# The experts' weighted rows: gather, multiply and add on VectorE, or multiply on ScalarE and add in the scatter

## What is computed

```python
xt = hn.reshape(N, D)                       # N = 1024 tokens, D = 1024
g_sel = jnp.argmax(g_logits, axis=-1)       # one of 4 groups
top_val, top_loc = lax.top_k(e_in, TOP_K)   # 2 of its 8 experts
gates = jax.nn.softmax(top_val, axis=-1) * g_gate
...
hb = jax.nn.silu(xb @ w_e_gate[e]) * (xb @ w_e_up[e])      # (rows, 256)
return (hb @ w_e_down[e]).astype(jnp.float32) * wts[:, None]
...
out = jnp.zeros((N + 1, D), jnp.float32).at[tok_buf].add(yb.reshape(P, D))[:N]
```

## Time and profile before

| | us |
|---|---|
| time, median of 3 runs (lowest to highest) | 1071.8 (1071.31 to 1072.05) |
| the profiled execution's own time | 1072.77 |
| its span in the profile | 1070.9 |
| TensorE busy | 971.1 (91%) |
| VectorE busy | 774.2 (72%) |
| ScalarE busy | 464.9 (43%) |
| GpSimd busy | 325.7 (30%) |

### The profile page before, as it was taken

The page is one execution under the profiler, slowest core; times in us unless marked ns, Lnnn a source line. Parts: engine busy times, 40 slices in busy tenths (PEclk is TensorE's granted clock), DMA queues, the critical chain, the costliest instruction groups (busy, mean ns, idle before and its releaser), DMA issues.

```text
span 1070.9 us, 13353 instructions
## 1 busy us (share of the span) xinstructions
PE 971.1 (91%) x4709; PEld 757.7 (71%) x4709; DVE 774.2 (72%) x1265; ACT 464.9 (43%) x812; POOL 325.7 (30%) x339
## 2 busy tenths in 40 slices
PE   5998989888889798999998999975999999999993
PEld 4776766556677676668876888864777777777772
DVE  5647776887787577883256677687888888888881
ACT  5234452223344423332034343343666676667650
POOL 2234114321441322210021111014245554555422
PEclk9999998998999898999999999986999999999997
DMA  7232233112232422516020111675899999999981
GB/s 250 70 92 78 92 126 99 60 59 79 80 99 89 157 90 97 159 59 226 20 85 20 40 60 60 260 293 193 334 374 399 402 400 408 408 402 405 406 287 57
DMA packets 63395, 197.38 MB, mean 184 GB/s; under 512 B 16416, under 2 KB 22976, under 8 KB 50912
## 3 DMA queue, kind: packets, MB, share of 16 engines
q1 hardware_dynamic: 43344, 152.73, 38.7%
q0 software_dynamic: 18688, 39.52, 10.4%
q10 hardware_dynamic: 1296, 4.26, 1.0%
HBM read 190.17 MB, written 37.75 MB: 213 GB/s over the span
## 4 chain that ended last, share of the span: by engine, by line
PE 67%; DVE 16%; issue 9%; ACT 2%; POOL 2%; DMA 1%; SPq 0%; ACTq 0%; DVEq 0%; POOLq 0%
PE bank L953 10%; PE bank L954 9%; PE bank L955 9%; PE gu_ps L953 5%; PE gu_ps L955 5%; PE gu_ps L954 5%; PE y_ps L1335 5%; PE xg_ps L1300 3%; DVE Wl L1778 2%; PE bank L1024 2%; PE bank L1227 1%; PE y_ps L955 1%; PE y_ps L954 1%; PE y_ps L953 1%; PE bank L1112 1%
## 5 line engine op out<-in xcount | busy, mean ns | idle before, releaser
L953 PE MATMUL bank<-Wh,hTh 128*128 128x512 f32 x384 | 156.2, 407 | 0.0
L1761 DVE TENSOR_TENSOR egl<-egr,ghi 128x2048 fp32r<-128x2048 f32 x64 | 143.9, 2288 | 14.2 <-ACT ghi L1405 14.2
L954 PE MATMUL bank<-Wl,hTh 128*128 128x512 f32 x384 | 151.0, 393 | 0.0
L955 PE MATMUL bank<-Wh,hTl 128*128 128x512 f32 x384 | 151.0, 393 | 0.0
L1405 ACT ACTIVATE ghi<-egr 128x2048 fp32r<-128x2048 f32 x64 | 119.7, 1934 | 0.0
L953 PE MATMUL gu_ps<-ghi,xgH 128*128 128x512 f32 x256 | 104.3, 408 | 1.4 <-DVE xgL L2143 1.4
L955 PE MATMUL gu_ps<-ghi,xgL 128*128 128x512 f32 x256 | 101.5, 396 | 0.0
L954 PE MATMUL gu_ps<-egl,xgH 128*128 128x512 f32 x256 | 101.0, 395 | 0.0
L953 PEld LDWEIGHTS bank<-Wh,hTh 128*128 128x128 f32 x384 | 73.5, 191 | 16.5 <-issue 2.1
L955 PEld LDWEIGHTS bank<-Wh,hTl 128*128 128x128 f32 x384 | 73.0, 190 | 15.9
L2475 POOL DMA_INDIRECT partial_rows<-pg,idh x28 | 47.5, 1695 | 119.9 <-DVE pg L2168 119.9
(11 more groups left out here) (328 smaller groups left out, 2092.8 us busy)
## 6 DMA issues: line engine op xcount, KB each, us to landing
egr<-w_e_gate SPq DMA_DIRECT2D x32, 1024.0 KB
egr<-w_e_up SPq DMA_DIRECT2D x32, 1024.0 KB
edr<-w_e_down SPq DMA_DIRECT2D x32, 1024.0 KB, 12.5
raw<-w_in SPq DMA_DIRECT2D x50, 256.0 KB, 3.0
xn<-w_in SPq DMA_DIRECT2D x22, 256.0 KB, 2.9
x_sb<-x_prompt SPq DMA_DIRECT2D x8, 512.0 KB, 6.0
partial_rows<-x_sb ACTq DMA_DIRECT2D x8, 512.0 KB, 2.7
raw<-w_xkv SPq DMA_DIRECT2D x14, 256.0 KB, 3.7
```

What stands on the lines that cost most here:

```text
L953: pe.matmul(dst, ah, bh, start=first, stop=False)
L954: pe.matmul(dst, ah, bl, start=False, stop=False)
L955: return pe.matmul(dst, al, bh, start=False, stop=last)
L1761: tt(egl[n % 4][:, a, :, :], egr[n % 4][:, a, :, :], ghi[n % 2][:, a, :, :].bitcast(F32), ALU.subtract)\
```

## The change

`add_rows` leaves VectorE. ScalarE gets `weigh_rows(n-1)`, between hidden_silu(n) and down_high(n+1), and once more at the end: it writes y_ps times the gate into `pg`, without an addend. `gather_sums` is gone. `store_rows` and `out_rows` scatter with `compute_op=ALU.add`, so that the DMA adds the rows to what stands in DRAM. Since two experts that lie four apart share tokens, the scatter of expert n waits on GpSimd until that of expert n-4 has landed; `weigh_rows(n)` waits for the same before it overwrites the buffer.

```diff
--- before.py
+++ after.py
@@ -569,7 +569,6 @@
         g_used = sem("g_used")
         d_used = sem("d_used")
         xg_ld = [sem(f"xg_ld{i}") for i in range(3)]
-        pg_ld = [sem(f"pg_ld{i}") for i in range(4)]
         xg_full = sem("xg_full")
         xg_high = sem("xg_high")
         xg_low = sem("xg_low")
@@ -1662,6 +1661,15 @@
                 copy(hbF[:, :], hb_ps[:, P:2 * P])
                 copy(hbH[:, 0, :], hb_ps[:, 0:P]).then_inc(hb_high, 1)
 
+            def weigh_rows(n):
+                e = expert(n)
+                if n == 0:
+                    act.wait_ge(meta_done, 1)
+                act.wait_ge(d_used, n + 1)
+                if n > 3:
+                    act.wait_ge(px_st[n % 4], 16 * (n // 4))
+                copy(pg[n % 4][:, :], y_ps[:, :], scale=gate_s[:, e:e + 1]).then_inc(ey_done, 1)
+
             down_high(0)
             act.wait_ge(ids_done, 1)
             act.wait_ge(g_in, 1)
@@ -1680,9 +1688,11 @@
                     gate_high(n + 1, 0)
                     gate_high(n + 1, 1)
                 hidden_silu(n)
+                weigh_rows(n - 1)
                 if n + 1 < NE:
                     down_high(n + 1)
             hidden_high(NE - 1)
+            weigh_rows(NE - 1)
 
             def more_first():
                 act.wait_ge(g_used, NE)
@@ -2159,15 +2169,6 @@
                 dve.wait_ge(hb_high, n + 1)
                 tt(hbL[:, 0, :], hb_ps[:, 0:P], hbH[:, 0, :].bitcast(F32), ALU.subtract).then_inc(hb_low, 1)
 
-            def add_rows(n):
-                e = expert(n)
-                if n == 0:
-                    dve.wait_ge(meta_done, 1)
-                dve.wait_ge(d_used, n + 1)
-                dve.wait_ge(pg_ld[n % 4], 16 * (n // 4 + 1))
-                stt(pg[n % 4][:, :], y_ps[:, :], gate_s[:, e:e + 1], pg[n % 4][:, :], ALU.mult, ALU.add)\
-                    .then_inc(ey_done, 1)
-
             def gate_values():
 
                 dve.wait_ge(g_exp, 1)
@@ -2232,7 +2233,6 @@
                     gate_low(n + 1, 0)
                     gate_low(n + 1, 1)
                 hidden(n)
-                add_rows(n - 1)
                 if n + 1 < NE:
                     down_low(n + 1)
                 if n == 2:
@@ -2240,7 +2240,6 @@
                 if n == 3:
                     half_rows()
             hidden_low(NE - 1)
-            add_rows(NE - 1)
 
             def more_first():
 
@@ -2471,6 +2470,11 @@
                                                in_offset=bass.IndirectOffsetOnAxis(ap=idx, axis=0),
                                                bounds_check=bound, oob_is_err=False)
 
+            def add_rows(table, idx, frm, bound):
+                return pool.indirect_dma_start(out=table, out_offset=bass.IndirectOffsetOnAxis(ap=idx, axis=0), in_=frm,
+                                               in_offset=None, bounds_check=bound, oob_is_err=False,
+                                               compute_op=ALU.add)
+
             def spread_rows(table, idx, frm, bound):
                 return pool.indirect_dma_start(out=table, out_offset=bass.IndirectOffsetOnAxis(ap=idx, axis=0), in_=frm,
                                                in_offset=None, bounds_check=bound, oob_is_err=False)
@@ -2481,24 +2485,20 @@
                     pool.wait_ge(xg_full, 2 * n - 4)
                 fetch(xg[n % 3][:, :], hn_dram, idh[:, e:e + 1], last_row).then_inc(xg_ld[n % 3], 16)
 
-            def gather_sums(n):
-                e = expert(n)
-                if n > 3:
-                    pool.wait_ge(px_st[n % 4], 16 * (n // 4))
-                fetch(pg[n % 4][:, :], px_dram, idh[:, e:e + 1], last_row).then_inc(pg_ld[n % 4], 16)
-
             def store_rows(n):
                 e = expert(n)
                 pool.wait_ge(ey_done, n + 1)
-                spread_rows(px_dram, idh[:, e:e + 1], pg[n % 4][:, :], last_row).then_inc(px_st[n % 4], 16)
+                if n > 3:
+                    pool.wait_ge(px_st[n % 4], 16 * (n // 4))
+                add_rows(px_dram, idh[:, e:e + 1], pg[n % 4][:, :], last_row).then_inc(px_st[n % 4], 16)
 
             def out_rows(n):
                 e = expert(n)
                 pool.wait_ge(ey_done, n + 1)
                 pool.wait_ge(copied, 16 * NT)
                 pool.wait_ge(halves_done, 1)
-                spread_rows(out[0][0], idp[:, e:e + 1], pg[n % 4][:, :], last_half).then_inc(out_st, 16)
-                spread_rows(out[1][0], ids[:, e:e + 1], pg[n % 4][:, :], last_half).then_inc(out_st, 16)
+                add_rows(out[0][0], idp[:, e:e + 1], pg[n % 4][:, :], last_half).then_inc(out_st, 16)
+                add_rows(out[1][0], ids[:, e:e + 1], pg[n % 4][:, :], last_half).then_inc(out_st, 16)
 
             pool.wait_ge(ids_done, 1)
             gather_rows(0)
@@ -2506,8 +2506,6 @@
             for i in range(NT):
                 pool.wait_ge(x_st[i % TPS], 16 * (i // TPS + 1))
             gather_rows(2)
-            for n in range(4):
-                gather_sums(n)
             gather_rows(3)
             gather_rows(4)
             for n in range(1, NE):
@@ -2515,8 +2513,6 @@
                     store_rows(n - 2)
                 if n + 4 < NE:
                     gather_rows(n + 4)
-                if 2 < n < NE - 1:
-                    gather_sums(n + 1)
             for n in range(NE - 4, NE):
                 out_rows(n)
             pool.wait_ge(out_st, 16 * 8)
```

## The result

The changed kernel took 1078.74 us (median; 1078.46 to 1081.39), the kernel before 1071.55 beside it: ratio 1.0073, 95% interval 1.0051 to 1.0094. Two further measurements gave 1.0066 (1.0047 to 1.0086) and 1.0102 (1.0083 to 1.0122). So it is 0.8% slower, some 9 us; +12.8 us was forecast. The profiled execution took 1081.39 us.

The account below looks back on a forecast made before the run. TensorE, busy all 50.00 of 50 us in mid-loop, was taken to set the pace, with transfers beside it at their limit. Loop +10.0 and tail +2.8 gave +12.8 over the median 1071.8: 1084.6 us, range 1072 to 1099.

Parts of the forecast that it names:

- The chain and its room: Expert loop: from down's end through ScalarE's first ghi, egl twice and ehb to turn_hidden; ehb may be 0.26 us late.
- ScalarE's price: ScalarE's new 128x1024 operation, right behind down's end and ahead of dhi, delays the chain by 0.96 us (0.86 to 1.28).
- Every second expert: Expert loop: TensorE's stop of 0.70 us (0.60 to 1.02) returns at every second expert, as the next chain fits.
- H_2: Place of turn_hidden(2) behind the end of down(1); TensorE's first stop there, 0.70 us.
- H_3: Place of turn_hidden(3) behind down(2)'s end, in the period with VectorE's counts; a stop of 0.97 us, 0.79 before.
- Loop: All TensorE stops over the expert loop together: +10.0 us (8.7 to 14.1).
- The adding scatter at twice a plain one: Expert loop's transfers: an adding scatter costs 2 plain ones (bounds 1 and 4), taking what the gather gave back; term nothing.
- The steady landing: Expert loop: a sign of being right, the time edr's weight loads take to land stays steady.
- room for a factor of 2.5: Expert loop's transfers: at 402 GB/s an adding scatter may take 2.5 times a plain one.
- The rival in which transfers take over: Expert loop: adding scatter beyond a factor of about 2.8, weights come too late; 1106 us at factor 4; chance 13%.
- the tail: Kernel's end: dearer issues of the adding output scatters +1.5, their longer landing +1.3; +2.8 us (0 to about 8).
- The rival "not slower": Expert loop: VectorE paces the chain, so taking 1.28 us off it removes TensorE's stop; 1070.8 us; chance 13%.

Follow-up runs that it names:

- between the ghi, last six in place: Changed kernel with ScalarE's multiplication between the two ghi copies for experts 0 to 25, in the changed kernel's place for 26 to 31; ratio 1.0046.
- the transfers alone: Changed kernel's adding scatter without the gather of partial sums, but VectorE multiplies y_ps by the gate and ScalarE is as before; ratio 1.001.
- gather kept: Adding scatter with VectorE multiplying and ScalarE as before, plus the gather of partial sums kept, its data unused; ratio 1.0155.

## Why the prediction was right, and where it was off

- **The chain and its room: shown.** The 0.26 us of room was read from the single stop of the trace before. Three delays bear it out: 0.95 us gave 0.68 per stop, 0.54 us gave 0.25, and the multiplication moved between the two ghi, expected to stop 0.27, gave 0.34 (9.95+9.83 for 19.44).
- **ScalarE's price.** Taken as 0.96, measured 1.01 from the new operation to dhi; but it began 0.05 to 0.06 us sooner behind down's last matmuls than dhi had, so the net delay is 0.95.
- **Every second expert: shown.** The two periods together take 20.12 us against 19.44, so 0.68 per stop where 0.70 was forecast; H_2 0.63 for 0.70, H_3 1.03 for 0.97. Loop +9.7 against +10.0.
- **The adding scatter at twice a plain one: shown**, 2.05 by engine time. The guess from a gather plus a scatter was close by luck as much as by reason; no row before the change had it. The Trainium skill, Collectives: The Full Stack (The bandwidth ceiling), puts the price of a reducing transfer between ranks down to two source reads; the factor of 2.05 here agrees with that.
- **The steady landing: so, but by the slower loop.** edr's stays at 11 us. With the same transfers and a period of 9.72 it grows to 14.2 and 15.7, and the prediction's own sum leaves no room there: 3.13+0.26+2x0.26 = 3.91 MB, all that 402 GB/s move in 9.72 us. Its room for a factor of 2.5 was worked out for a period of 9.72+0.35. The rival in which transfers take over was nearer than its 13% suggests: it came with one gather more.
- **The failed term is the tail, +2.8 forecast and 0 to +0.3 measured.** The issue was even dearer than taken (1.55 for 1.30), and the last one ends 10.25 behind H_31 where it was 8.97, +1.3. But the time from store(27)'s issue to the copies was shorter, not longer: 1031.64 to 1036.34, 4.7 us where it was 7.5. The term had priced the adding and taken the rest of the landing as before. But how long a transfer takes to land follows from the loop's pace. The kernel with a 128x1024 copy more on ScalarE shows it; it gathers and scatters as before and is only slower:

```profile
1032.74 1.01 POOL L2478 DMA_INDIRECT partial_rows<-pg,idh  x1 [8.02 <-DVE pg L2171]
```

```profile
1036.07 2.50 SPq L934 DMA_DIRECT2D y_prompt<-partial_rows  x4
```

There it is 3.3 us. All kernels, in the order of edr's landing (us):

| kernel | H_1 to H_31 | landing of edr, 950 to 1000 | store(27) to the copies |
|---|---|---|---|
| copy 128x1024 more | 301.3 | 9.5 | 3.3 |
| changed, plain scatters | 301.2 | 9.8 | 4.1 |
| changed | 301.3 | 11.3 | 4.7 |
| copy 128x512 more | 295.4 | 11.3 | 4.2 |
| between the ghi, last six in place | 296.6 | 12.5 | 6.9 |
| between the ghi | 296.0 | 13.0 | 5.6 |
| before | 291.6 | 14.2 | 7.5 |
| the transfers alone | 291.6 | 14.2 | 6.9 |
| dhi on VectorE | 291.2 | 15.7 | 7.8 |
| gather kept | 302.5 | 23.8 | 13.2 |

The adding itself costs 0.6 of the 4.7 (4.1 with plain scatters); dropping the gather is not what shortened it, since the kernel with the copy keeps it. So the copies started earlier against H_31 (22.6 us for 18.7), GpSimd waited 1.27 us for the last multiplication, and the dearer issues lay in that room. The kernels with the transfers alone and with dhi on VectorE, whose loop is as fast as before and whose copies start 19.6 and 18.9 us ahead, do pay 1 to 3 us. The term would have been near its mark if the loop had not lost time: loop and tail don't add up independently. The other part is behind the last issue: 10.4 us to the end where it was 11.5, although the adding output scatters land 3.9 to 4.2 us after their issue and the plain ones 2.4 to 2.5 (second trace of the kernel before). It is also 10.5 with plain scatters, so it is not the adding; what it is stays open.
- **The rival "not slower"** fell as reasoned: VectorE's 1.28 us came back as waiting (2.4 us for dhi, then again 0.5 for ghi), and no engine could use them.

No version beat the kernel before. Both that repair the loop (multiplication on VectorE, or dhi there) are level with it: TensorE then fills each period, and the change has nothing that shortens TensorE's work.

## What to carry to other kernels

Before moving work to the engine with the lower busy share, look for the chain from one event of the bounding engine to the next, and at which link the idle engine waits: idle time that lies ahead of the event doesn't hold work that needs the event. A delay in a chain that spans two periods shows up in every second one, and its room can be read from the single place where the trace already stops. And price the end with its queue, and with the loop's loss put in: the same scatter cost nothing or 3 us, depending on when the copies before it could start, and a slower loop lets them start earlier.

## What the runs showed of the hardware that was not expected

- The adding scatter takes GpSimd 1.55 us to issue where a plain one takes 0.97, with a quiet VectorE. In the loop it took 1.59 in the changed kernel and a median of 2.1 to 2.5 with dhi on VectorE, with the transfers alone and with the multiplication between the ghi; the plain one took 1.74 in the kernel before and 1.01 when put into the changed kernel.
- From 800 to 1000 the DMA share reads 1.01 at 364 GB/s (adding) as at 403 (before), and 0.97 with plain scatters at 365. The bytes counted don't tell an adding scatter from a plain one; that they leave out what the addition reads is inferred. Nor did a share of 1.01 say that the transfers bind: it was 1.01 in the kernel before too, where TensorE was busy 200.00 of these 200 us.
- The rounding copy of 128x1024 from SBUF to SBUF took 0.69 us on VectorE and 1.05 to 1.06 on ScalarE.
- TensorE's stops of 0.4 us in the records (0.7 in the period) left the granted clock at 1.00.
